# Context tiles' output products of layer 0 moved from the mixing stage into the expert stage, with a ring of six rows there

## What is computed

```python
def _mix_out(p, o, gdn_norm, dw_w, dw_b, gn_w, gn_b, w_out, rows):
    ...
    return jnp.concatenate([y_gdn, y_f, y_c], axis=-1) @ w_out

def _peer(h, wq, keys, u_tab, v_tab):
    ...
        act = jax.nn.gelu(jnp.einsum("tkd,td->tk", u_tab[eb], hb))
        return jnp.einsum("tk,tkd->td", gb * act, v_tab[eb])

def _layer(...):
    ...
    x = x + gt1 * mix(p, o, rows)
    x = x + gt2 * peer(_rms(x, norm2) * (1 + sc2) + sh2)
    if not last:
        xc = xc + cgt1 * mix(pc, oc, None)
        xc = xc + cgt2 * peer(_rms(xc, norm2) * (1 + csc2) + csh2)
    return x, xc
```

## Time and profile before

| | before |
|---|---|
| median of 3 runs | 4367.65 us (4362.76 to 4370.74) |
| the profiled execution | 4369.42 us, its span 4367.4 us |
| mean granted clock of TensorE | 0.975 |
| TensorE / VectorE / ScalarE / GpSimd busy | 85% / 69% / 39% / 38% |
| expert stage of layer 0, first dot to first dot of the held tile | 665.8 to 2310.9 us |

### The profile page before, as it was taken

The page is one execution under the profiler, slowest core; times in us unless marked ns, Lnnn a source line. Parts: engine busy times, 40 slices in busy tenths (PEclk is TensorE's granted clock), DMA queues, the critical chain, the costliest instruction groups (busy, mean ns, idle before and its releaser), DMA issues. The chain is left out here.

```text
span 4367.4 us, 55136 instructions
## 1 busy us (share of the span) xinstructions
PE 3697.2 (85%) x18945; PEld 1905.5 (44%) x18945; DVE 3006.2 (69%) x6251; ACT 1721.1 (39%) x5272; POOL 1647.7 (38%) x1508
## 2 busy tenths in 40 slices
PE   7998998988888888888886788889898888887777
PEld 3566854433433433433432334775443343343222
DVE  3964567876776775875875886457797687687444
ACT  2223623444344344344342454343444433433333
POOL 0004503444443444444443442352444444444332
PEclk9999999999999999999998999899999999999999
DMA  8360159999999999999999998014999999999997
GB/s 340 117 243 26 37 198 372 421 420 420 410 416 422 410 420 419 409 419 421 407 417 366 408 388 305 2 37 180 418 421 421 421 419 421 421 408 421 422 421 327
DMA packets 238985, 1506.07 MB, mean 345 GB/s; under 512 B 28433, under 2 KB 33617, under 8 KB 71153
## 3 DMA queue, kind: packets, MB, share of 16 engines
q0 software_dynamic: 184320, 1342.26, 74.6%
q1 hardware_dynamic: 54384, 160.28, 9.8%
HBM read 1490.32 MB, written 12.12 MB: 344 GB/s over the span
## 5 line engine op out<-in xcount | busy, mean ns | idle before, releaser
L2851 PE MATMUL ps<-low,pediag 128*128 128x512 f32 x2180 | 1066.0, 619 | 231.6 <-ACT pediag L2760 225.0
L2623 DVE CUSTOM_DVE_ANT_0 low<-low,hc 128x1024 f32<-128x1024 f32 x545 | 667.9, 1225 | 371.2 <-DMA low<-in_experts_dram,eid 356.0
L2602 POOL DMA_INDIRECT low<-in_experts_dram,eid x537 | 588.0, 1095 | 823.9 <-PE ps L2851 809.3
L2752 ACT ACTIVATE low<-peact 128x1 f32<-128x1 f32 x1152 | 232.0, 201 | 1389.7 <-DVE peact L2623 1388.5
L2851 PEld LDWEIGHTS ps<-low,pediag 128*128 128x128 f32 x2180 | 390.0, 193 | 835.6 <-ACT pediag L2760 514.4
L2760 ACT ACTIVATE pediag<-cst,low 128x128 f32<-128x128 f32 x1152 | 462.5, 401 | 42.5 <-PE ps L2851 5.1
L2755 ACT ACTIVATE low<-low,gw 128x1 f32<-128x1 f32 x1152 | 339.1, 294 | 37.4
L2851 PE MATMUL ps<-wide_a,pediag 128*128 128x512 f32 x640 | 307.2, 610 | 55.0 <-ACT pediag L2760 54.7
L2060 PEld LDWEIGHTS ps<-qkvT,arena 128*128 128x128 f32 x2560 | 315.6, 195 | 77.1 <-issue 77.1
L2851 PE MATMUL ps<-wide_b,pediag 128*128 128x512 f32 x640 | 302.8, 604 | 45.0 <-ACT pediag L2760 44.7
L2060 PE MATMUL ps<-qkvT,arena 128*128 128x128 f32 x2560 | 316.2, 277 | 2.4 <-ACT qkvT L2024 2.4
(11 more groups left out here) (502 smaller groups left out, 5779.8 us busy)
## 6 DMA issues: line engine op xcount, KB each, us to landing
pjdot<-in_mod_t_dram SPq DMA_DIRECT2D x64, 512.0 KB, 5.3
arena<-in_w_mod_dram SPq DMA_DIRECT2D x24, 1024.0 KB, 11.8
arena<-in_peer_wq_dram SPq DMA_DIRECT2D x8, 2048.0 KB, 17.1
low<-in_experts_dram,eid POOLq DMA_INDIRECT x609, 15.2
pjw<-in_w_cols_dram SPq DMA_DIRECT2D x18, 512.0 KB, 3.7
plw<-in_w_cols_dram SPq DMA_DIRECT2D x18, 512.0 KB, 8.2
qkvT<-mod_rows SPq DMA_DIRECT2D x9, 512.0 KB, 11.1
arena<-in_w_z_dram SPq DMA_DIRECT2D x2, 2112.0 KB, 12.4
```

The costliest lines, as they stand in the source:

```text
L2602: nc.gpsimd.indirect_dma_start(ring.row(g), None, table, bass.IndirectOffsetOnAxis(eid[:, j % 2, k:k + 1], 0)).then_inc(ring.landed(g), 16)
L2623: nc.vector.tensor_tensor_reduce(out=dot_out if final else ring.row(g)[:, 0:D], in0=ring.row(g)[:, 0:D], in1=hc[:, j % 2, :], scale=1.0, s ...
L2752: nc.scalar.activation(ge[:, g % 2, 0:1], act_v[:, j % 2, k:k + 1], ACT.Gelu_apprx_tanh).then_inc(gelu_ready, 1)
L2851: last = nc.tensor.matmul(ps[:, half, :], diag[:, g % DIAGS, :], ring.row(g)[:, D + half * 512:D + (half + 1) * 512], start=k == 0, stop=k ...
```

## The change

In layer 0, `mix_out` makes products for the four latent tiles alone (HALVES is 8) and stores their rows. The context tiles' products move into tile 0 of `peer`: SyncE streams the output weights again, in 16 pieces of 128x512 into two buffers in `dot_out`, and brings the context rows and the gate in halves into row 7; TensorE multiplies one piece for both context tiles at slots 40, 46, ... 82 and 94, 98, ... 122; VectorE gates and adds at slots 85, 87, 124 and 126; SyncE stores the halves, waits for the stores, and goes on. The three loads of the next layer's gains now come behind the last piece. The ring of layer 0 has six rows, 5, 6, 2, 3, 0, 1, for all five tiles; row 4 goes to the held tile, whose rows are now 4, 3, 5, 6, 2.

```diff
-    def place(self, g):
-        return (g - 1) % self.size
+        self.begun = 1 + (len(short) or len(order))
+        self.at = [None] + [short[(g - 1) % len(short)] if g <= until else order[(g - 1) % len(order)]
+                            for g in range(1, NT * SLOTS)]
...
+    def used_by(self, g):
+
+        return max((n for n in range(1, g) if self.at[n] == self.at[g]), default=None)
...
-    HALVES = 2 * len(tiles)
     EARLY = 4
+    HALVES = 2 * EARLY
...
-                for i in range(2, n_tiles):
+                for i in range(2, EARLY):
                     store(sp, i - 2)
...
-                store(sp, n_tiles - 2)
-                store(sp, n_tiles - 1)
+                store(sp, EARLY - 2)
+                store(sp, EARLY - 1)
...
+                early = min(ring.begun, ring.size)
+                for g in range(early):
                     if g:
-                        pool.wait_ge(prod_ready, products_reading(ring.order[ring.place(g)]))
+                        pool.wait_ge(prod_ready, products_reading(ring.at[g]))
...
+    W_AT, W_STEP, W_ADD = (40, 94), (6, 4), (85, 124)
...
-                if ahead:
+                def late_rows(half):
+
+                    sp.dma_start(late_row(0), mod_row(kit, L, 0, 2)[:, half_cols(half)]).then_inc(late_in, 16)
+                    for a, t in enumerate(late):
+                        sp.dma_start(late_row(1 + a), kit.ctx[0, t * P:(t + 1) * P, half_cols(half)]).then_inc(late_in, 16)
...
+                def late_piece_in(n):
+
+                    if n < 2:
+                        sp.wait_ge(sc.h_ready, 1)
+                    else:
+                        sp.wait_ge(late_used, n - 1)
+                    half, k = divmod(n, KD)
+                    sp.dma_start(piece_of(n), w_out_half(kit, L, half)[:, k, :]).then_inc(piece_in[n % 2], 16)
+
+                def late_loads():
+
+                    late_rows(0)
+                    for n in range(KD + 2):
+                        late_piece_in(n)
+                    late_store(0)
+                    for n in range(KD + 2, KD + 4):
+                        late_piece_in(n)
+                    sp.wait_ge(late_stored, 32)
+                    late_rows(1)
+                    for n in range(KD + 4, 2 * KD):
+                        late_piece_in(n)
                     for a, src in enumerate((kit.mod_d[L + 1, 1, D:2 * D], kit.mod_d[L + 1, 1, 0:D], kit.norm1[L + 1, :])):
                         sp.dma_start(n1[:, a, :], src.rearrange("(k p) -> p k", p=P),
                                      allow_slow_non_contiguous=True).then_inc(n1_in, 16)
+                    late_store(1)
+                    sp.wait_ge(late_stored, 64)
...
+                    if late and i == 0:
+                        late_loads()
...
-                    pool.wait_ge(summed, g - ring.size + 1)
+                    before = ring.used_by(g)
+                    if before is not None:
+                        pool.wait_ge(summed, before + 1)
...
+                def late_add(k):
...
+                        nc.vector.tensor_tensor(late_row(3), ps[:, 2 + a, :], late_row(0), ALU.mult).then_inc(late_gated, 1)
+                        dve.wait_ge(late_gated, n + 1)
+                        nc.vector.tensor_tensor(late_row(1 + a), late_row(1 + a), late_row(3), ALU.add).then_inc(late_sum, 1)
...
-                        if ahead and (i, k) == (0, 60):
+                        if ahead and (i, k) == (1, 20):
                             next_gain()
...
+                def late_products(k):
...
+                        pe.wait_ge(piece_in[at % 2], 16 * (at // 2 + 1))
+                        for a, t in enumerate(late):
+                            last = nc.tensor.matmul(ps[:, 2 + a, :], mixT[:, n, t, :], piece_of(at),
+                                                    start=n == 0, stop=n == KD - 1)
+                        last.then_inc(late_used, 1)
...
-HELD_ROWS = [5, 6, 2, 3, 4]
+HELD_ROWS = [4, 3, 5, 6, 2]
+SHORT_UNTIL = NT * SLOTS
...
-                ring = RowRing(first_row, rows, [5, 6, 2, 3, 4, 0, 1, 7], sems[0:RING + 1])
+                ring = RowRing(first_row, rows, [5, 6, 2, 3, 4, 0, 1, 7], sems[0:RING + 1], [5, 6, 2, 3, 0, 1], SHORT_UNTIL)
```

More of the change, by code:

```diff
@@ L2216, in products_reading @@
                 return 1
-            here = [i for i in range(n_tiles) if tiles[i] // 2 == row - 4]
+            here = [i for i in range(EARLY) if tiles[i] // 2 == row - 4]
             return 2 * (max(here) + 1) if here else 1
@@ L2405, in add @@
                         dve.wait_ge(x_in[i % 2], 16 * (i // 2 + 1))
-                        dve.wait_ge(gates_in, 16 + 16 * sum(i >= n for n in turns))
+                        dve.wait_ge(gates_in, 16)
                     dve.wait_ge(prod_ready, q + 1)
@@ L2458, in _, with peer @@
                         bass.IndirectOffsetOnAxis(kit.eid[:, 0, g:g + 1], 0)).then_inc(ring.landed(g), 16)
[L2459 to L2467, removed]
+                for g in range(early, ring.begun):
+                    for b in range(2):
+                        pool.wait_ge(stored[b], 16)
+                    nc.gpsimd.indirect_dma_start(
+                        ring.row(g), None, kit.experts.rearrange("l e d -> (l e) d"),
+                        bass.IndirectOffsetOnAxis(kit.eid[:, 0, g:g + 1], 0)).then_inc(ring.landed(g), 16)
+def peer(nc, kit, L, tiles, here, mixT, qkvT, ring, room, held, stored):
     N, M = len(tiles), here
@@ L2528, in peer @@
         steps = lambda i: range(SLOTS if i < M else R_AT + 1)
+        late = [] if final else [t for t in tiles if t < NC]
+        piece_in = (lw0, lw1)
+        piece_of = lambda n: dot_out[:, (n % 2) * 512:(n % 2 + 1) * 512]
+        late_row = lambda a: ring.rows[7][:, a * 512:(a + 1) * 512]
+        half_cols = lambda half: slice(half * 512, (half + 1) * 512)
         def mixed_rows(eng):
             for b in range(2):
-                eng.wait_ge(stored[b], 16 * ((N + 1 - b) // 2))
+                eng.wait_ge(stored[b], 32)
         with nc.Block(no_gpsimd_drain=bool(held)) as block:
@@ L2594, in _ @@
             def _(pool):
-                for g in range(ring.size + 1, SLOTS * M):
+                for g in range(ring.begun, SLOTS * M):
                     j, k = divmod(g, SLOTS)
@@ L2608, in _ @@
                 for g in range(HELD_RING if held else 0):
-                    if g:
-                        pool.wait_ge(summed, ring.last_slot(HELD_ROWS[g - 1], SLOTS * M) + 1)
+                    last = ring.last_slot(HELD_ROWS[g - 1], SLOTS * M) if g else None
+                    if last is not None:
+                        pool.wait_ge(summed, last + 1)
+                    elif g:
+                        pool.wait_ge(late_used, 2 * KD)
                     held.gather(g)
@@ L2734, in _ @@
                             late_piece(k)
+                        if late and i == 0:
+                            late_add(k)
                         if i < M and i + 1 < N:
@@ L2859, in piece @@
                             pe.wait_ge(n1_copied, j - 2)
+                        if late and j == 2:
+                            pe.wait_ge(late_gated, 4)
                         sc.turn_h(j)
@@ L2885, in _ @@
                             late_piece(k)
+                        if late and i == 0:
+                            late_products(k)
                         if i < M and i + 1 < N:
@@ L2990, in backbone @@
                         low[:, LOW_Y:LOW_Y + D], ring, sems[-2:])
[L2991 removed]
+                peer(nc, kit, 1, order, len(order), mixT, qkvT, ring, low[:, LOW_Y:LOW], None, sems[-2:])
 def constants():
```

62 lines of the change are left out of this document (41 added, 21 removed).

## The result

Over five runs each, the changed kernel takes 4389.6 us at the median (4384.66 to 4393.33), the kernel before 4366.9 (4362.76 to 4370.74): 22.7 us more, a ratio of 1.0048 with a 95% interval of 1.0035 to 1.0061. The forecast was 4385 us, slower; the measured time lies inside its range.

What follows compares the result with a forecast made beforehand. Transfers (expert-row gathers) set the pace in the expert stage, TensorE ahead of it. Terms: -24.4 + 16.3 + 2 + 7 + 16 = +17 on 4369.42 us, so 4386; with the median 1.8 lower, 4385 us, range 4362 to 4401.

Steps and rivals of the forecast that it cites:

- A: Start of layer 0's expert stage: gather 3 issues earlier, first dot at 641.4 in place of 665.8, -24.4 us.
- B: Tile 0: 6.82 MB of added transfers stand in line at 418 GB/s, +16.3 us (11.7 to 17.4).
- C: Tile 0: context products and sums come in bunches on TensorE and VectorE, partly uncovered by queued gathers, +2 us (0 to 8).
- D: Tiles 1 to 4: with six rows for eight, gathers come late at narrow places, +7 us (0 to 12).
- E: Tile 1: tile 2's row fetch waits behind slow gain loads and stores, so ScalarE and VectorE stand, +16 us (0 to 21).
- the wait of ScalarE: Slot 8 of tile 1: one ScalarE wait of about 20 us on the row's load.
- Tiles 2 to 4 within 3 us of 327: Sign that the forecast is right: these later tiles of the expert stage stay within 3 us of 327.
- rival 2: All five tiles: six rows starve, gathers needing nearer 8.9 us than 5.9, 4 us more per tile, 4405; chance 0.08.
- Rival 3: Tile 0: TensorE becomes the bound, 315 of 340 us busy, and may fall behind by 10 us, 4396; chance 0.06.
- from there gathers follow as now: Tile 0: after gather 7, issued near 650 when slot 1's sums end, gathers keep their present pace.
- -23 if the six-row ring costs one wait at the start: Start of tile 0: one end of the early start's gain, -23 us in place of -24.4.
- Rival 1: Tile 1: no stall, gain loads done some 40 us after 963, not 61; 4369 us, chance 0.24.

Runs made afterwards that it cites:

- run 9: Kernel before, ring of eight, with 26 more loads of 262 KB (6.82 MB) in tile 0, read by nothing: 4382.53 us, ratio 1.0037.
- run 10: Kernel of run 7 (ring of six) with the same 26 loads of 262 KB in tile 0 as run 9: 4393.2 us, ratio 1.0063.
- run 1: Changed kernel with the fetch of tile 2's row issued behind the first two pieces, ahead of gain loads and stores of halves: 4373.4 us, ratio 1.0014.
- run 4: Run 1 with eight rows in place of six from slot 22 of tile 1 on, held tile's rows as before the change: 4365.17 us, ratio 0.9997.
- run 7: Kernel before with layer 0's ring cut to six rows and held tile rows 4, 3, 5, 6, 2; products and loads stay: 4378.49 us, ratio 1.0040.
- run 5: Run 1 without the loads of 14 of the 16 weight pieces, all matmuls kept on the first two pieces: 4366.63 us, ratio 1.0003.
- run 6: Run 1 with all loads, but context products of 12 of 16 pieces cut to 32 columns of one tile: 4377.25 us, ratio 1.0029.
- run 2: Changed kernel with the three gain loads back at the head of the stage, tile 2's fetch still behind the stores: 4374.56 us, ratio 1.0017.
- run 3: Changed kernel with gain loads of the same bytes read as 128 contiguous pieces in place of 1024 per load: 4374.15 us, ratio 1.0015.
- run 8: Run 4 with the first gate half and context rows' halves (0.79 MB) loaded behind the third piece of weights: 4364.66 us, ratio 1.0002.

## Why the prediction was right, and where its terms were off

| term | forecast | measured | from |
|---|---|---|---|
| A, the early start | -24.4 | -23.8 | first dot, mean of 8 executions with the early start 643.5, of 4 without 667.3 |
| B, bytes in tile 0 | +16.3 | +17.6 | run 9, tile 0 |
| C, engines in tile 0 | +2 | +0.9 | changed kernel less run 10, tile 0 |
| D, six rows | +7 | +12.3 | 4.3 in tile 0 (run 10 less run 9), 8.0 in tiles 1 to 4 (run 1 less run 4) |
| E, the fetch behind the gain loads | +16 | +15.7 | tile 1, changed kernel less run 1 |
| sum | +17 | +22.7 | medians: +22.7 |

That the sum meets the medians to a tenth is luck: each row is good to a microsecond or two. That the forecast's own sum lies 5.7 us lower is term D's 5.3 for the most part.

Of the signs that the prediction named, the first dot (644.24 for 641), tile 0 (22.8 us longer for 20), the gain loads (60.7 us), the wait of ScalarE (18.09), tile 1 (345.4) and its DMA share (0.97) came. Tiles 2 to 4 within 3 us of 327 did not (326.4, 331.4 and 336.5), but the kernel before has 327.3, 330.8 and 332.3 there; only tile 4 is longer by 4 us, where rival 2 wanted all three.

- **A** held by its own steps. Gather 3 was forecast at 636.9 and the first dot at 641.4; the profiled execution has 639.69 and 644.24, but its products ended 2.8 us later too (gather 2 at 638.45 for 635.63), and over the eight executions the first dot lies between 640.9 and 644.9.
- **B** came out a little over its upper end of 17.4 in run 9, where loads alone come in. That every byte stands in line holds for the sum of run 9 and not byte by byte: under six rows the same bytes cost 13.5 us (run 10 less run 7), and the 14 pieces of run 5 4.8 us where the line gave 8.8.
- **C** held as a net of the whole tile, 0.9 us, within the spread of one execution; the 4 us at dots 84 to 88 show that the engines' bunches do hold the dots, and part of that is made up by the end. Its upper end was given as a third of 27.6, which is 9.2 and not 8; nothing hung on it. Rival 3 fell with run 6.
- **D** was the mis-sized term: 12.3 for 7, at its upper end of 12. The step that failed was to take one narrow place in tiles 1 to 4 and leave tile 0 out. Gather 7 was issued 8.9 us after the first dot, forecast 8.6, but "from there gathers follow as now" did not hold: two gathers fewer were under way, and six rows cost 4.5 us by dot 30 and 8.4 us in that tile alone (run 7). The forecast's "-23 if the six-row ring costs one wait at the start" saw this wait and gave it 1.4 us. For tiles 1 to 4 the estimate of 5.6 and some more was about right: 6.0 in run 7 and 8.0 between runs 1 and 4. Over all profiled executions, these tiles take 1325.1 us on average with six rows (runs 1, 2, 3, 5, 6, 7 and 10, from 1319.4 to 1328.4) and 1317.9 with eight (the kernel before, runs 4, 8 and 9, from 1316.7 to 1319.7), 7.2 more; between runs 9 and 10 alone there is no difference. Rival 2's 4 us in every tile did not come.
- **E** held step by step. Forecast: gain loads issued at 963 to 964, landed at 1024, stores by 1029.5, the fetch landed at 1037.8, a wait of 21 us. Traced: issued from 962.06, the last landed 60.7 us after 964.78, at 1025.5; fetch issued at 1031.71, square at 1035.81, a wait of 18.09 us. Run 1 takes the wait away, run 2 clears the stores, run 3 shows that the number of pieces is the cause. Rival 1 asked for loads that drain in some 40 us; they did not. That the Trainium skill's rule of turns by packets would bring rival 1 was wrong: the prediction set one gather packet of 0.283 us against each turn, where the rule's turn holds several (behind run 3).
- One sentence was wrong at no cost: the held tile's first row is not free from the start. It lies in the memory that also holds the query weights (`kit.arena`, line 3060), so its gather waits for the last queries.

What stays open: without 14 pieces (run 5) tile 0 lost 4.8 us, where 3.67 MB at run 10's price (13.5 us for 6.82 MB) would be 7.3. By the table most of the gain shows behind dot 88; ahead of it VectorE's gates and sums hold the dots in run 5 as in run 1. Whether these, TensorE's products and the waits of the six rows leave gaps that the early loads fill is argued, and no run takes them apart.

No version tried beats the kernel before: run 4 (0.9997) and run 8 (1.0002) are level with it. They show what the idea is worth once its slip and the missing rows are mended: the early start gives 23.8 us, and the bytes and six rows of tile 0 take 22 back (17.6 and 4.3).

## What to carry to other kernels

Price a load of single numbers by its pieces and not by its bytes where it runs beside large packets: here three loads of 4 KB held a queue for 61 us. Before a transfer is moved, look at what will stand behind it in its program and who waits for that; here one fetch put ahead was worth 16 us. Fewer buffers are priced first at the place where the pipeline fills, and work moved from an idle stretch of the transfers into a full one pays there for most of its bytes: what the start gained here, the full stage took back.

## What the runs showed of the hardware that was not expected

- A transposed load of 1024 numbers counted as 1024 packets, and each of an engine's 64 took about the time of one gather packet beside gathers (about 19 us a load for 64 x 0.283 = 18.1): 60.7 us for three loads beside gathers, 9.7 at the head of the stage (run 2), 13.7 as 128 packets each beside gathers (run 3).
- With six rows in flight in place of eight, tile 0's transfers moved 403 GB/s in place of 418 at nearly the same busy share (1.00 for 1.01, run 7): here the busy share does not show the short queue, and the GB/s do. In tiles 1 to 4 the six rows kept 412 to 416 GB/s.
